# High and low inputs of a projection in one 512-column matmul, with the low sums apart

## The reference

```
first:  x = layer_norm(ALPHA * x + mixer(x), g, b)        # mixer A, then mixer B
second, for layer in 0, 1:
    hn = rms_norm(h);  h = h + mixer(hn)                  # z = hn @ w_in; ...; @ w_out
    h = h + cross_attention(rms_norm(h), m, wq, wkv, wo)  # q = h @ wq, ..., o @ wo
    z = rms_norm(h) @ w_up;  u, g = z[:, :2048], z[:, 2048:]
    h = h + (gelu(dwconv3(g) + b) * u) @ w_down
return rms_norm(h)
```

## Time and profile before

| | us |
|---|---|
| median of 3 runs | 1037.66 |
| lowest, highest | 1037.25, 1040.43 |
| profiled execution, own time | 1037.87 |
| its span, first to last instruction | 1036.1 |
| TensorE busy | 1011.9 |
| VectorE busy | 664.6 |
| ScalarE busy | 530.3 |
| mean granted TensorE clock | 0.995 of full |

### The profile page before, as it was taken

How to read it: one execution, slowest core, us unless ns; L and a number is a source line. 1 busy time by engine, 2 the same in 40 slices (tenths; PEclk the granted TensorE clock), 3 DMA queues, 4 the chain that set the end, 5 groups by cost and what they waited for, 6 DMA issues and landing times.

```text
span 1036.1 us, 18469 instructions
## 1 busy us (share of the span) xinstructions
PE 1011.9 (98%) x7450; PEld 945.6 (91%) x7450; DVE 664.6 (64%) x1022; ACT 530.3 (51%) x804; POOL 165.8 (16%) x146
## 2 busy tenths in 40 slices
PE   9999899999999999999999999999999999999996
PEld 7779669999978998888999999999998999999996
DVE  4779675754457678566456569755576655658852
ACT  4547473454477455455345447544354545436641
POOL 0001022300026231001002005210034200103500
PEclk9999999999999999999999999999999999999998
DMA  9634415465440536425514554447546433455431
GB/s 357 228 122 163 160 45 203 163 221 185 168 157 2 200 141 228 179 88 204 197 45 162 200 203 162 163 176 270 203 163 237 151 141 122 166 200 175 150 122 40
DMA packets 24971, 172.56 MB, mean 167 GB/s; under 512 B 2768, under 2 KB 2896, under 8 KB 4432
## 3 DMA queue, kind: packets, MB, share of 16 engines
q1 hardware_dynamic: 23328, 160.86, 43.4%
q10 hardware_dynamic: 1584, 10.88, 2.7%
HBM read 166.49 MB, written 5.24 MB: 166 GB/s over the span
## 4 chain that ended last, share of the span: by engine, by line
PE 79%; DVE 9%; ACT 5%; issue 3%; DMA 1%; POOL 1%; SPq 1%; POOLq 0%; DVEq 0%; ACTq 0%
PE bank L428 54%; PE bank L499 14%; DVE wl L1354 3%; ACT wh L904 2%; DVE work L1731 2%; PE bank L624 2%; PE bank L578 1%; DMA raw<-w 1%; PE bank L606 1%; POOL acc L1846 1%; DVE work L1734 1%; PE bank L626 1%; PE bank L542 1%; ACT work L1271 1%; PE bank L701 1%
## 5 line engine op out<-in xcount | busy, mean ns | idle before, releaser
L1354 DVE TENSOR_TENSOR wl<-raw,wh 128x1024 fp32r<-128x1024 f32 x300 | 385.1, 1291 | 241.0 <-ACT wh L904 239.9
L904 ACT ACTIVATE wh<-raw 128x1024 fp32r<-128x1024 f32 x300 | 311.9, 1054 | 284.9 <-PE bank L428 221.9
L428 PE MATMUL bank<-xh,wh 128*128 128x256 f32 x1152 | 320.1, 285 | 0.0
L428 PE MATMUL bank<-xh,wl 128*128 128x256 f32 x1152 | 318.0, 283 | 0.0
L428 PE MATMUL bank<-xl,wh 128*128 128x256 f32 x1152 | 295.7, 284 | 0.0
L428 PEld LDWEIGHTS bank<-xh,wl 128*128 128x128 f32 x1152 | 221.3, 192 | 0.3
L428 PEld LDWEIGHTS bank<-xh,wh 128*128 128x128 f32 x1152 | 221.1, 192 | 0.3
L428 PE MATMUL bank<-yh,wh 128*128 128x256 f32 x768 | 209.0, 285 | 0.8 <-ACT yh L1275 0.8
L428 PEld LDWEIGHTS bank<-xl,wh 128*128 128x128 f32 x1152 | 207.8, 192 | 0.1
L428 PE MATMUL bank<-yh,wl 128*128 128x256 f32 x768 | 207.0, 283 | 0.0
L428 PE MATMUL bank<-yl,wh 128*128 128x256 f32 x768 | 178.4, 283 | 1.4 <-DVE yl L1749 1.4
(11 more groups left out here) (173 smaller groups left out, 1120.2 us busy)
## 6 DMA issues: line engine op xcount, KB each, us to landing
raw<-w SPq DMA_DIRECT2D x149, 1024.0 KB, 4.8
k_scratch<-kt ACTq DMA_DIRECT2D x2, 1024.0 KB, 8.6
kt<-k_scratch ACTq DMA_DIRECT2D x2, 1024.0 KB, 6.1
h<-xt SPq DMA_DIRECT2D x4, 256.0 KB, 5.8
raw<-w SPq DMA_DIRECT2D x2, 512.0 KB, 5.6
cs<-cst SPq DMA_DIRECT2D x1, 1024.0 KB, 12.4
v<-memt ACTq DMA_DIRECT2D x1, 1024.0 KB, 7.5
m_scratch<-yh ACTq DMA_DIRECT2D x1, 1024.0 KB, 3.9
```

The source lines that it names most:

```text
L428: return pe.matmul(b[:, j, :], weights, o_[:, kk, :], start=k0 + k == 0 and q == 0 and (j == 0 or not both_open), stop=k0 + k == KT * p.de ...
L904: act.activation(wh[:, n % 2, j, :], raw[:, n % RAW_SLOTS, j, :], ACT.Copy).then_inc(hi_ready, 1)
L1354: dve.tensor_tensor(wl[:, n % 2, j, :], raw[:, n % RAW_SLOTS, j, :], wh[:, n % 2, j, :].bitcast(F32), ALU.subtract).then_inc(lo_ready, 1)
```

## The change

The inputs xh, xl become two halves of one tensor `xx` (yh, yl of `yy`), the eight banks one tensor `banks`. Phases marked `apart` (oa, ob, qn, kn, oab, cb, cc, oc, ox, fu, fd) give each half of an output a bank of its own: the first 256 columns take the sums of `wh*xh` and `wl*xh`, the other 256 those of `wh*xl`. Where the chunk isn't early, `wh` times high and low input is one matmul of 512 columns, its moving operand being two strips of 256; `wl*xh` stays one of 256. An early chunk keeps three matmuls. An output takes two banks, outputs take turns over all four, and a phase behind such a one waits for the last output but one; the second output of an `apart` phase also waits for the whole phase before.

Evacuation has two parts. In residual phases VectorE adds the main sums to h and then, when that is written, the low sums. In fu, qn, kn, cb, cc ScalarE copies the low sums to the destination, VectorE adds the main sums and multiplies by rb. kx, gb, qb, kb, ga, qx, cu and fg stay as they were.

Two broadcasts move: that of the memory norm from the last chunk of ga behind the first half chunk of va (its `spread` behind one more `hi`), that of mix0 in zf behind the first token tile of the second half of chunk 1.

```diff
-        p.wide = wide
-        p.pair = 2 * (len(order) % 2)
+        p.wide, p.apart = wide, apart
+        p.prev = order[-1] if order else None
         p.before = order[-2] if len(order) >= 2 else None
+
+
+        p.pair = 0 if p.prev is None else p.prev.pair if p.prev.apart else 2 - p.prev.pair
...
-    add("oa", 4, "dve")
+    add("oa", 4, "dve", apart=True)
...
-    add("qn", 2, "dve")
-    add("kn", 2, "dve")
+    add("qn", 2, "dve", apart=True)
+    add("kn", 2, "dve", apart=True)
...
+        xx = sb("xx", [P, 2, KT, S], F32R)
+        yy = sb("yy", [P, 2, 2 * KT, S], F32R)
+        xh, xl = [xx[:, q, :, :] for q in range(2)]
+        yh, yl = [yy[:, q, :, :] for q in range(2)]
...
-        bank = [ctx.enter_context(nc.psum_tensor(f"bank{i}", [P, 512], F32)) for i in range(8)]
+        banks = ctx.enter_context(nc.psum_tensor("banks", [P, 8, 512], F32))
+        bank = [banks[:, i, :] for i in range(8)]
...
+        def apart(p, o):
+
+            q = p.pair ^ 2 * (o % 2)
+            return banks[:, q:q + 2, 0:S], banks[:, q:q + 2, S:2 * S]
...
             def enter(p):
 
-                if p.before is not None:
+                if p.prev is not None and p.prev.apart:
+                    pe.wait_ge(evac[p.prev.reader], p.prev.end - 1)
+                elif p.before is not None:
                     pe.wait_ge(evac[p.before.reader], p.before.end)
...
+                        if p.apart:
+                            b = banks[:, p.pair ^ 2 * (c // p.deep):, :]
+                            if c == p.deep:
+                                pe.wait_ge(evac[p.prev.reader], p.prev.end)
...
+                            if p.apart:
+                                at = slice(S, 2 * S) if q == 2 else slice(0, S)
+                                return pe.matmul(b[:, j, at], weights, o_[:, kk, :], start=k0 + k == 0 and q == 0,
+                                                 stop=k0 + k == KT * p.deep - 1 and q == 2, skip_group_check=True)
...
+                        def apart_product(k, j):
+
+                            pe.matmul(b[:, j, :], wh[:, slot, j, k * P:k * P + P], operand[:, :, tile0 + k0 + k, :],
+                                      start=k0 + k == 0, stop=False, skip_group_check=True)
+                            return pe.matmul(b[:, j, 0:S], wl[:, slot, j, k * P:k * P + P], oh[:, tile0 + k0 + k, :],
+                                             start=False, stop=k0 + k == KT * p.deep - 1, skip_group_check=True)
...
-                                for q in range(2 if early else 0, 3):
-                                    mm = product(k, q, j)
+                                if p.apart and not early:
+                                    mm = apart_product(k, j)
+                                else:
+                                    for q in range(2 if early else 0, 3):
+                                        mm = product(k, q, j)
...
-                                         (2, 1, 3): lambda: stats("mem"), (3, 1, 4): lambda: bcast("mem")})
+            project("ga", xx, hooks={(1, 0, 2): then((turn_unit, 8)), (1, 1, 3): then((turn_unit, 9)),
+                                         (2, 1, 3): lambda: stats("mem")})
...
-                (0, 1, 1): first_scores, (1, 0, 1): second_scores, (2, 0, 1): lambda: score_pair(4, 5),
+                (0, 0, 1): lambda: bcast("mem"), (0, 1, 1): first_scores, (1, 0, 1): second_scores, (2, 0, 1): lambda: score_pair(4, 5),
...
-            project_tokens("zf", xh, xl, x_ready("mix0"), {(0, 1, 1): lambda: stats("mix0"), (1, 0, 1): lambda: bcast("mix0")})
+            project_tokens("zf", xh, xl, x_ready("mix0"), {(0, 1, 1): lambda: stats("mix0"), (1, 1, 0): lambda: bcast("mix0")})
...
+                    if low is not None:
+                        act.wait_ge(w_used, 2 * n + 2)
+                        act.activation(low[:, 2 * c:2 * c + 2, :], apart(p, c)[1], ACT.Copy).then_inc(low_out, 1)
...
-                (0, 0): lambda: spread("mem", rb_m), (1, 1): lambda: exponentials("A", 0),
+                (0, 1): lambda: spread("mem", rb_m), (1, 1): lambda: exponentials("A", 0),
...
-            chunks("qn")
-            chunks("kn")
+            chunks("qn", low=qz)
+            act.wait_ge(k_saved, 32)
+            chunks("kn", low=kt)
...
+                            main, low = apart(p, o)
+                            if alpha is None:
+                                chain(dve.tensor_tensor(hc, main, hc, ALU.add))
+                            else:
+                                chain(dve.scalar_tensor_tensor(hc, hc, alpha, main, ALU.mult, ALU.add))
+                            dve.tensor_tensor(hc, low, hc, ALU.add).then_inc(dve_evac, 1)
+                        elif alpha is None:
...
-            def times_rb(dst, name=None):
+            def times_rb(dst, name=None, low=None):
 
                 def f(c, b):
                     if c == 0 and name is not None:
                         dve.wait_ge(rb_ready, RBS[name] + 1)
-                    dve.tensor_tensor(dst[:, 2 * c:2 * c + 2, :], b, rb[:, :].unsqueeze(1).broadcast_to([P, 2, S]),
-                                      ALU.mult).then_inc(dve_evac, 1)
+                    d = dst[:, 2 * c:2 * c + 2, :]
+                    if low is not None:
+                        dve.wait_ge(low_out, LBASE[low] + c + 1)
+                        chain(dve.tensor_tensor(d, b[0], d, ALU.add))
+                        b = d
+                    dve.tensor_tensor(d, b, rb[:, :].unsqueeze(1).broadcast_to([P, 2, S]), ALU.mult).then_inc(dve_evac, 1)
```

More of the change, by code:

```diff
@@ L77, in schedule, with add @@
     order = []
-    def add(name, chunks, reader, outs=None, deep=1, wide=False):
+    def add(name, chunks, reader, outs=None, deep=1, wide=False, apart=False):
         nonlocal at
@@ L114, in schedule @@
     add("attN", 0, "dve", 4)
-    add("oab", 4, "dve")
+    add("oab", 4, "dve", apart=True)
     for l in "01":
         if l == "1":
-            add("cb", 4, "dve")
-            add("cc", 4, "dve")
+            add("cb", 4, "dve", apart=True)
+            add("cc", 4, "dve", apart=True)
             add("cu", 4, "dve")
@@ L166 @@
 GEBASE = bases(("ffn0", 8), ("ffn1", 8))
+LBASE = bases(("qn", 2), ("kn", 2), ("fu0", 8), ("cb", 4), ("cc", 4), ("fu1", 8))
 STAT = bases(*[(u, 1) for u in ("mem", "mean0", "var0", "mean1", "var1", "mix0", "xa0", "ffn0", "mix1", "xa1",
@@ L397, in enter, with project @@
             def enter(p):
-                if p.before is not None:
+                if p.prev is not None and p.prev.apart:
+                    pe.wait_ge(evac[p.prev.reader], p.prev.end - 1)
+                elif p.before is not None:
                     pe.wait_ge(evac[p.before.reader], p.before.end)
-            def project(name, oh, ol, ready=None, hooks={}, tile0=0):
+            def project(name, operand, ready=None, hooks={}, tile0=0):
                 p = PH[name]
+                oh, ol = [operand[:, q, :, :] for q in range(2)]
                 enter(p)
@@ L904, in hi, with chunks @@
                 act.activation(wh[:, n % 2, j, :], raw[:, n % RAW_SLOTS, j, :], ACT.Copy).then_inc(hi_ready, 1)
-            def chunks(name, evacuate=None, split=0, last=None, hold=False, skip=0, between={}):
+            def chunks(name, evacuate=None, split=0, last=None, hold=False, skip=0, between={}, low=None):
                 p = PH[name]
@@ L1328, in _ @@
                 residual("ox" + l, "ffn" + l, "ffn" + l)
-                chunks("fu" + l, spreading("ffn" + l))
+                chunks("fu" + l, spreading("ffn" + l), low=qz)
                 products("ffn" + l, "fg" + l, l)
@@ L1370, in chunks @@
                         dve.wait_ge(w_used, 2 * n + 2)
-                        evacuate(c // p.deep, b3(p.pair + c // p.deep % 2))
+                        evacuate(c // p.deep, apart(p, c) if p.apart else b3(p.pair + c // p.deep % 2))
                     if between is not None:
@@ L1698, in _ @@
             chunks("zf", between=bias, split=1)
-            chunks("qn", times_rb(qz, "mix0"), between=lambda c: bias(2 + c))
+            chunks("qn", times_rb(qz, "mix0", low="qn"), between=lambda c: bias(2 + c))
             dve.wait_ge(k_saved, 32)
-            chunks("kn", times_rb(kt))
+            chunks("kn", times_rb(kt, low="kn"))
             chunks("vn", hold=True)
@@ L1780, in _ @@
                     inverse_rms("mix1", RMS_EPS)
-                    chunks("cb", times_rb(qz, "mix1"), split=1)
-                    chunks("cc", times_rb(kt))
+                    chunks("cb", times_rb(qz, "mix1", low="cb"), split=1)
+                    chunks("cc", times_rb(kt, low="cc"))
                     def scaled(c, b):
@@ L1813, in _ @@
                 inverse_rms("ffn" + l, RMS_EPS)
-                chunks("fu" + l, times_rb(qz, "ffn" + l), split=1)
+                chunks("fu" + l, times_rb(qz, "ffn" + l, low="fu" + l), split=1)
                 dve.wait_ge(padded, 4 + 4 * int(l))
```

60 lines of the change are left out of this document (28 added, 32 removed).

## The result

| | before | after |
|---|---|---|
| median, us | 1037.80 (8 runs) | 1046.01 (8 runs) |
| lowest, highest | 1036.99, 1040.43 | 1043.37, 1053.44 |
| profiled execution, its span | 1037.87, 1036.1 | 1045.71, 1043.9 |

The ratio is 1.0084, with a 95% interval of 1.0060 to 1.0108: slower by 0.8%, where no clear change and 1036.0 us were forecast, and outside the range.

A forecast was written before the change was run, and what follows sets the result against it. TensorE, busy 98%, was taken as the bound. Against 1037.87 us, -7.9 - 4.6 - 1.35 + 8.3 + 1.5 + 0.7 gave 1034.5, plus 1.7 for one slow clock 1036.2 (median 1036.0); range 1027.5 to 1041.

The forecast's parts named there:

- The merge: In 38 chunks, 512 plus 256 columns replace three matmuls of 256, 0.347 for 0.360 us: 7.9 us of TensorE time saved.
- The moves: Moved broadcasts end TensorE's stops: 4.6 us at ga and va, slow clock included, and 1.35 us in zf.
- Rival (c): Moved broadcasts fail: the wait returns at the first scores, or VectorE is late with va's weights; 1041.9 us, chance 0.06.
- Low sums and second evacuation at nothing: In qn, kn, cb, cc and fu, ScalarE's copies and VectorE's additions are hidden: no cost; 20 us without that cover.
- The ring: Residual phases: 0.70 us more per output stops TensorE 2.7 us at fu0, qx1, fu1 (8.3 together), 1.5 in vx0.
- oa's and ob's norms: The sum before these norms waits, but TensorE's mean comes over 1 us later: nothing taken, at most 0.7 us twice.
- The slow clock: One of the three new TensorE stops is followed by granted clock 0.50, costing 1.7 us.
- The end: Nothing hides the last second addition before the square, final norm and output: 0.7 us longer.
- Rival (a): Stops shrink to under 1 us each without slow clock, so the gains come through: 1027.5 us, chance 0.25.
- Rival (b): The merged matmul is no cheaper than two, 0.240 us: 1043.9 us, slower; chance 0.09.

The follow-up runs named there:

- the first experiment: Kernel after with no phase apart, only the two broadcasts still moved: 1032.75 us, ratio 0.9949 to the kernel before.
- the second experiment: Kernel after with oa, ob, oab, oc, ox0 and ox1 as before the change, the other marked phases still apart: 1030.06 us, ratio 0.9924.
- the run with one strip: Kernel after with the merged matmul's moving operand in one contiguous strip of 512 (two tiles of the high input): 1054.72 us, run once.
- square last: Kernel after with ScalarE's square in the residual phases moved behind the second weight conversion: 1033.08 us, ratio 0.9952.
- fill: Kernel after plus ten 512-column matmuls into an unused bank at the start of fu0, qx1 and fu1: 1042.63 us, ratio 1.0045.

## Why the prediction was wrong, step by step

- **The merge** (7.9 us): it measured 5.4. The mechanism was right and the term too large; the pair was costed from rows where each length follows its own kind, and in 23 chunks or more the alternation costs 6 ns a pair more. The measured gain lies between the bounds that were named (nothing at 0.240 us, 7.9 + 6.7 us at 0.216). But 0.216 us was no bound: the score matmuls that it comes from have 256 columns, as their rows show (L578, 128x256), and their inputs aren't of the type fp32r.
- **The moves** (4.6 + 1.35): measured 4.5 and 1.5 (1.4 in the first experiment). Right, the stretch of slow clock included. Rival (c) is refuted.
- **Low sums and second evacuation at nothing** in qn, kn, cb, cc, fu: right, the second experiment shows it.
- **The ring** (2.7 us at each of three phases, 1.5 in vx0): right in place, cause and size. The stops without their clock come to 2.9 in fu0, and vx0 lost 1.7. The count of eight rows of one phase gave the period within 0.04 us.
- **oa's and ob's norms** ("I take nothing, at most 0.7 twice"): this step failed most. It cost 1.1 + 2.7 = 3.8 us. I gave the delay as one addition, 0.7 us against more than 1 us of slack (1.3 in the trace before). It was 2.3 us. A delay changes who comes first: the subtraction got ahead of GpSimd's sum and slowed it from 1.29 to 2.12 us, and VectorE was 0.7 us late already, since its subtraction before (2.32 us) had met a sum too. The same wait of one for the other stood in the earlier trace rows, where the subtraction took 1.91 us in place of 1.15 behind the sum; I used it in the ring and did not ask where else it would turn.
- **The slow clock** (one of three stops, 1.7 us): there were three stretches, one twice as long, and one of them behind a stop in kx1 that the forecast did not have. qx1 and fu1 lost 3.9 + 5.8 - 2 x 2.9 = 3.9 us to it, and kx1 1.6 of its 2.7.
- **The end** (0.7): right. The last L461 starts at 1030.87 and L577 at 1033.41, 2.54 us; before 1.82.

The forecast missed by 1045.7 - 1036.2 = 9.5 us for the profiled execution: 3.8 of the norms (1.6 of it clock), 3.9 - 1.7 = 2.2 of the clock behind the ring's stops, 2.5 of the merge, 0.2 of vx0, 0.3 of the three stops (8.6 in place of 8.3) and 0.5 of small things, 9.5 in all. No single one would have taken it out of the range; that the first three leaned the same way did. Rival (a), the ring yields, is refuted. Rival (b), the merged matmul costs two plain ones, is refuted too (a pair takes 0.347 or 0.353 us, not 0.360), though its doubt was in place.

## What to carry to other kernels

Operations of 0.7 us on an engine that is busy for two thirds of the time, 32 of them or 22 us, can cost 17 us, if they stand in loops of dependences that only just keep pace; so follow one turn of such a loop through all engines before adding to it, and look for what can leave the loop (here one square) before giving up the idea. When a step comes later, ask not only whether its slack covers the delay but which instruction of another engine it now meets, and who starts first. Count each stop of over 2 us of TensorE as a risk of slow clock; behind the stops of fu0, qx1 and fu1 it cost from nothing to 4.2 us in these traces. And take the gain of a merged instruction from a row of the mixture that will run, not from rows of each kind alone.

## What the runs showed of the hardware

- Next to each other, GpSimd's sum and VectorE's subtraction of SBUF operands don't share: the one that started second stretched from 1.29 to 2.12 us, or from 1.22 to 2.11.
- The same stop had very different sequels: behind the stop of 2.4 us in fu0 the clock stayed at 1.00 in the change and was at 0.50 for 10.3 us in the run with one strip; in fu1 it was at 0.50 for 6.8 us in the change and for 3.4 us without `apart` in oa and ob. A stop of 1.16 us ahead of the norm's products (eight matmuls of one column, 0.9 us) was followed by 0.50 in kx1 and not in kx0, in each of the four traces that have it (the change, square last, fill, one strip). What decides isn't shown. Longer runs of one kernel are those with more of it: the run of 1053.44 us had a mean granted clock of 0.983, the other seven of the change 0.988 to 0.993.
- A matmul of 512 columns that alternates with one of 256 runs on one of two levels for nearly a whole chunk: 0.230 + 0.117 us for each pair, or three pairs in turn of 0.236 + 0.114, 0.232 + 0.118 and 0.240 + 0.120 us. In a row of its own kind the 512 settles at 0.227 us after the first five or six, the 256 at 0.120.
